# MLP of a decoder trunk: one more half product joined in the first stage, and the order of VectorE's additions in the last chunks

## The reference

```
def _squared_relu_mlp(h, w1, w2):
    return jnp.square(jax.nn.relu(h @ w1)) @ w2
for layer in range(DEPTH):           # DEPTH = 2
    h = _rms_norm(x, norm_mix_g[layer])
    x = x + mixer(h)                 # attention in layer 0, retention in layer 1
    h = _rms_norm(x, norm_ffn_g[layer])
    x = x + _squared_relu_mlp(h, ffn_w_in[layer], ffn_w_out[layer])
return _rms_norm(x, final_g)
```

## Time and profile before

| | us |
|---|---|
| median of 3 runs (1245.33 to 1245.84) | 1245.82 |
| the profiled execution, its own time | 1246.04 |
| its span, first to last instruction | 1244.2 |
| TensorE busy (PE), share of the span | 1233.8, 99% |
| VectorE busy (DVE) | 983.8, 79% |
| ScalarE busy (ACT) | 779.0, 63% |
| POOL busy | 297.0, 24% |

### The profile page before, as it was taken

How to read it: one execution, slowest core, us unless ns; L and a number is a source line. 1 busy time by engine, 2 the same in 40 slices (tenths; PEclk the granted TensorE clock), 3 DMA queues, 4 the chain that set the end, 5 groups by cost and what they waited for, 6 DMA issues and landing times.

```text
span 1244.2 us, 18372 instructions
## 1 busy us (share of the span) xinstructions
PE 1233.8 (99%) x6870; PEld 1064.4 (86%) x6870; DVE 983.8 (79%) x1280; ACT 779.0 (63%) x1088; POOL 297.0 (24%) x330
## 2 busy tenths in 40 slices
PE   9999999999999999999999999999999999999997
PEld 6788888898888988889898889898889888898886
DVE  6588647598889798898666797567898988979888
ACT  6688755477575675765656645556677747466474
POOL 2343653111211112101131212231231122111220
PEclk9999999999999999999999999999999999999999
DMA  7367567778988989874968597969589898889983
GB/s 246 98 135 165 134 152 193 206 204 195 226 212 229 228 184 231 216 224 111 226 138 188 137 232 170 220 153 233 99 224 245 209 202 218 228 221 210 226 202 107
DMA packets 147976, 238.89 MB, mean 192 GB/s; under 512 B 51104, under 2 KB 72872, under 8 KB 147888
## 3 DMA queue, kind: packets, MB, share of 16 engines
q0 software_dynamic: 32352, 102.79, 44.0%
q1 hardware_dynamic: 115232, 134.60, 34.1%
q10 hardware_dynamic: 304, 0.33, 0.1%
HBM read 127.57 MB, written 2.11 MB: 104 GB/s over the span
## 4 chain that ended last, share of the span: by engine, by line
PE 87%; DVE 6%; issue 2%; ACT 2%; DMA 1%; SPq 0%; POOLq 0%; POOL 0%; ACTq 0%; DVEq 0%
PE banks L1072 19%; PE banks L1452 11%; PE banks L1030 11%; PE banks L998 6%; PE banks L1520 6%; PE banks L1241 6%; PE banks L1041 6%; PE banks L1401 5%; PE banks L1181 4%; PE banks L1035 3%; PE banks L1466 2%; PE banks L1343 2%; PE banks L1208 2%; DVE w L2356 2%; PE banks L1415 1%
## 5 line engine op out<-in xcount | busy, mean ns | idle before, releaser
L2356 DVE TENSOR_TENSOR w<-raw_tiles,w 128x1024 fp32r<-128x1024 f32 x312 | 371.7, 1220 | 33.8 <-ACT w L1662 33.8
L1662 ACT ACTIVATE w<-raw_tiles 128x1024 fp32r<-128x1024 f32 x312 | 316.3, 1052 | 129.6 <-PE banks L1072 60.8
L1072 PE MATMUL banks<-w,arena_q 128*128 128x512 f32 x1332 | 305.2, 390 | 0.7 <-DVE x L2696 0.7
L3378 POOL DMA_DIRECT2D raw_tiles<-raw_tiles x176 | 152.3, 905 | 629.9 <-DVE w L2356 358.1
L1072 PEld LDWEIGHTS banks<-w,arena_q 128*128 128x128 f32 x1332 | 248.7, 188 | 53.9 <-DVE x L2696 2.0
L1452 PE MATMUL banks<-w,h_ops 128*128 128x512 f32 x672 | 154.0, 390 | 0.0
L1452 PEld LDWEIGHTS banks<-w,h_ops 128*128 128x128 f32 x672 | 125.6, 188 | 25.7
L1030 PE MATMUL banks<-h_ops,w 128*128 128x512 f32 x576 | 144.1, 392 | 0.0
L1030 PEld LDWEIGHTS banks<-h_ops,w 128*128 128x128 f32 x576 | 104.0, 189 | 18.8
L1041 PEld LDWEIGHTS banks<-h_ops,w 128*128 128x128 f32 x576 | 78.6, 190 | 5.6
L998 PE MATMUL banks<-h_ops,w 128*128 128x256 f32 x672 | 82.0, 283 | 0.0
(11 more groups left out here) (253 smaller groups left out, 1886.3 us busy)
## 6 DMA issues: line engine op xcount, KB each, us to landing
raw_tiles<-raw_tiles POOLq DMA_DIRECT2D x176, 512.0 KB, 5.6
raw_tiles<-in_ffn_w_in SPq DMA_DIRECT2D x64, 512.0 KB, 6.2
raw_tiles<-in_ffn_w_out SPq DMA_DIRECT2D x64, 512.0 KB, 6.1
raw_tiles<-in_odd_w_in SPq DMA_DIRECT2D x32, 512.0 KB, 5.3
raw_tiles<-in_even_w_in SPq DMA_DIRECT2D x48, 256.0 KB, 3.5
raw_tiles<-in_odd_w_in SPq DMA_DIRECT2D x32, 256.0 KB, 5.5
raw_tiles<-in_odd_w_out SPq DMA_DIRECT2D x16, 512.0 KB, 6.0
raw_tiles<-raw_tiles POOLq DMA_DIRECT2D x20, 256.0 KB, 4.1
```

What stands on the lines that cost most here:

```text
L1072: mm = pe.matmul(bank[first + t][:, :], a_ring[a_slot(g, i)][:, a, k, P * t:P * t + P], w_slots[use_slot(use)][:, b, k, :], start=(starts ...
L1662: nc.scalar.activation(w_flat(use_slot(use), 0, half), raws[tile][:, 1024 * half:1024 * half + 1024], ACT.Copy).then_inc(m_hi, 1)
L2356: nc.vector.tensor_tensor(w_flat(use_slot(use), 1, half), raws[use_tile(key)][:, 1024 * half:1024 * half + 1024], w_flat(use_slot(use), 0, ...
L3378: pool.dma_start(raws[dst][:, part], raws[src][:, part], accum_op=ALU.add).then_inc(t_made[value][half], 16)
```

## The change

In the first stage, half b = 0 of product 5 is joined as well (`WIDE` now lists pairs of product and half). Its sums in HIGH come on top of those of products 0 and 4, so `wide_x_cross(HIGH, 0)` waits for product 5 and stands directly before `wide_x(HIGH, 0)`, behind two weight remainders, instead of between the two LOW instructions of half 0. The two semaphores of the cross subtractions become one, counted in the new order.

In the second stage of the last chunks (g = 3 and 7), product 4's tile 0 is added before product 3's two tiles, not after them. In g = 3, product 5's tile 0 is added before the remainder of the next stage's first weights and the variance, not after. ScalarE's square of the first tile waits for product 3's addition, now the later one.

```diff
+ADD_ORDER = [(i, t) for i in (0, 1, 4, 5, 2, 3, 6) for t in range(2)]
+LAST_ORDER = [(0, 0), (0, 1), (1, 0), (1, 1), (2, 0), (2, 1), (4, 0), (3, 0), (3, 1), (4, 1), (5, 0), (5, 1), (6, 0), (6, 1)]
 def add_order(g):
-    return (0, 1, 2, 3, 4, 5, 6) if g % CHUNKS == CHUNKS - 1 else (0, 1, 4, 5, 2, 3, 6)
+    return LAST_ORDER if g % CHUNKS == CHUNKS - 1 else ADD_ORDER
 def added(g, i, t=1):
-    return 14 * g + 2 * add_order(g).index(i) + t + 1
+    return 14 * g + add_order(g).index((i, t)) + 1
-def add_before(g, i):
-    same = [key for key in ADDS[:ADDS.index((g, i))] if PRODUCTS[key[1]][3] == PRODUCTS[i][3]]
+def add_before(g, i, t):
+    same = [key for key in ADDS[:ADDS.index((g, i, t))] if PRODUCTS[key[1]][3] == PRODUCTS[i][3] and key[2] == t]
...
-WIDE = (0, 1, 2, 3, 4, 6)
+WIDE = [(i, b) for i in range(7) for b in range(2) if (i, b) != (5, 1)]
...
-                            if i in WIDE:
+                            if (i, b) in WIDE:
...
-                    act.wait_ge(p_added, added(CHUNKS * (norm // 2) - 1, 4, t))
+                    act.wait_ge(p_added, added(CHUNKS * (norm // 2) - 1, 3 if t == 0 else 4, t))
...
             def wide_x_cross(g, tokens, b):
...
-                dve.wait_ge(p_done, use_done(first_use(g, 4), b))
-                nc.vector.tensor_tensor(v, v, wide_part(4, b, HIGH), ALU.subtract).then_inc(low_cross if low else high_cross, 1)
+                dve.wait_ge(p_done, use_done(first_use(g, 4 if low or b else 5), b))
+                nc.vector.tensor_tensor(v, v, wide_part(4, b, HIGH), ALU.subtract).then_inc(x_crossed, 1)
             def wide_x(g, tokens, b):
...
-                dve.wait_ge(low_cross if low else high_cross, wide_count(g) + b + 1)
+                dve.wait_ge(x_crossed, 2 * wide_count(g) + (b if low else 3 - b) + 1)
...
                     for b in range(2):
                         wide_x_cross(g, LOW, b)
-                        wide_x_cross(g, HIGH, b)
+                        if b == 1:
+                            wide_x_cross(g, HIGH, b)
                         wide_x(g, LOW, b)
                     w_lo(stage, 6, 1)
                     w_lo(stage + 1, 0, 0)
+                    wide_x_cross(g, HIGH, 0)
                     wide_x(g, HIGH, 0)
                     wide_x(g, HIGH, 1)
...
                 w_lo_both(stage + 1, 5)
+                add_product(g, 4, 0)
                 if last:
                     add_product(g, 3, 0)
                     add_product(g, 3, 1)
-                add_product(g, 4, 0)
                 operand_lo(g, 6)
                 add_product(g, 4, 1)
...
                 if norm == 2:
-                    use_lo(("qk", 0, 0), 0)
+                    add_product(g, 5, 0)
                 variance(norm, 0)
...
-                add_product(g, 5, 0)
+                use_lo(("qk", 0, 0), 0)
                 normed(norm, 0)
```

More of the change, by code:

```diff
@@ L235, in products_done @@
     return use_done(second_use(g, i), t)
+ADD_ORDER = [(i, t) for i in (0, 1, 4, 5, 2, 3, 6) for t in range(2)]
+LAST_ORDER = [(0, 0), (0, 1), (1, 0), (1, 1), (2, 0), (2, 1), (4, 0), (3, 0), (3, 1), (4, 1), (5, 0), (5, 1), (6, 0), (6, 1)]
 def add_order(g):
-    return (0, 1, 2, 3, 4, 5, 6) if g % CHUNKS == CHUNKS - 1 else (0, 1, 4, 5, 2, 3, 6)
+    return LAST_ORDER if g % CHUNKS == CHUNKS - 1 else ADD_ORDER
 def added(g, i, t=1):
-    return 14 * g + 2 * add_order(g).index(i) + t + 1
-ADDS = [(g, i) for g in range(2 * CHUNKS) for i in add_order(g)]
-def add_before(g, i):
-    same = [key for key in ADDS[:ADDS.index((g, i))] if PRODUCTS[key[1]][3] == PRODUCTS[i][3]]
+    return 14 * g + add_order(g).index((i, t)) + 1
+ADDS = [(g, i, t) for g in range(2 * CHUNKS) for i, t in add_order(g)]
+def add_before(g, i, t):
+    same = [key for key in ADDS[:ADDS.index((g, i, t))] if PRODUCTS[key[1]][3] == PRODUCTS[i][3] and key[2] == t]
     return same[-1] if same else None
@@ L711, in trunk @@
         z_added = sem("z_added")
-        low_cross = sem("low_cross")
-        high_cross = sem("high_cross")
+        x_crossed = sem("x_crossed")
         last_copied = sem("last_copied")
@@ L2688, in add_product @@
             def add_product(g, i, t):
-                if add_before(g, i):
-                    dve.wait_ge(p_added, added(*add_before(g, i), t))
+                if add_before(g, i, t):
+                    dve.wait_ge(p_added, added(*add_before(g, i, t)))
                 dve.wait_ge(p_done, products_done(g, i, t))
```

## The result

| | before | after |
|---|---|---|
| median of 21 runs each | 1245.49 (1244.95 to 1247.12) | 1247.6 (1246.91 to 1249.39) |
| the profiled execution's own time | 1246.04 | 1247.95 |
| its span | 1244.2 | 1246.1 |
| mean granted TensorE clock | 0.999 | 0.998 |

The ratio after to before is 1.0017, its 95% interval 1.001 to 1.0024: 2.1 us slower, with an interval of about 1.2 to 3.0. The forecast was 0.9 slower, 1246.7. The sign was right, but the slowdown is more than twice the forecast one: 1247.6 lies outside the forecast's own range (1246.2 to 1247.2) and at the very edge of the wide one (1245.3 to 1247.6). The kernel before came out at 1245.49 here, 0.33 lower than the 1245.82 on which the forecast stands. So it is the sizes that have to be looked for.

A forecast was written before the change was run, and what follows sets the result against it. TensorE's pace was taken to bound nearly everything, VectorE's chain the end from 1201.96. Terms 0.91 - 0.11 + 0.12 = +0.92 on 1245.82 gave 1246.7, own range 1246.2 to 1247.2, wide range 1245.3 to 1247.6.

The forecast's parts named there:

- VectorE's late pair: Before product 6: two dependent HIGH subtractions, starting 0.73 apart, hold TensorE, so product 6 really starts 0.15 later.
- TensorE's saved 0.09: Product 5 in each joined chunk: TensorE saves 0.08 to 0.09 if nothing holds it.
- the waits won in g = 3: Second stage: TensorE wins 0.9 before products 5 and 6, waits it off before the next norm's tile turn, keeps 0.11.
- the tail: From 1201.96 to the end: only VectorE's chain sets the length; the dependent pair of additions adds 0.12.
- rival A: Whole kernel: TensorE's own stalls are what counts, so removing them gives -2.1, 1243.7; chance 12%.
- Rival B: Dependent VectorE pairs cost no more than independent ones: +0.03 per joined chunk, total within 0.1 of 1245.8; chance 17%.
- covered behind: Into the second stage: the operand remainder slips 0.25, hidden by 0.5 of cover before the load.
- Rival C: Later subtraction spills into the second stage, each chunk paying 0.45 or more: +2.7, 1248.5; chance 6%.
- part 2: Fourth chunk (g = 3), reordered additions: `normed` starts 0.11 earlier, -0.11; bounds -0.93 and +0.12.
- paid six times: Product 6 in six joined chunks: the 0.15 delay recurs in each, +0.91 in all.
- part 3: Last chunk (g = 7), same reorder: only the dependent pair of additions counts, +0.12; bounds -0.3 and +0.2.
- part 1: Half of product 5 joined in six chunks: product 6 0.15 later each, +0.91; bounds -0.54 and +1.8.

The follow-up runs named there:

- e2: Kernel before with the new order of additions alone, product 5 not joined and the HIGH cross in its old place: 1246.16, ratio 1.0006.
- e8: e1 with six tiny VectorE instructions added at the start of VectorE's list: 1246.69, ratio 1.0007.
- e4: Changed kernel with the HIGH cross subtraction of half 0 moved between the two weight remainders, so one remainder splits the dependent pair: 1246.62, ratio 1.0009.
- e3: Changed kernel with the first tile's variance placed before product 5's addition in g = 3: 1246.65, ratio 1.0011.
- e1: Kernel before with half 0 of product 5 joined in six chunks, additions in the old order: 1247.06, ratio 1.0011.
- e7: e1 with 2 warm-up products instead of 9, meant to shift TensorE's instructions: 1248.06, ratio 1.0017.
- e9: Kernel before with the joined half alone, only in chunks g = 1, 2, 3 (layer 0): 1245.83, ratio 1.0003.
- e10: Kernel before with the joined half alone, only in chunks g = 5, 6, 7 (layer 1): 1246.16, ratio 1.0005.
- e5: Changed kernel with both HIGH subtractions of half 0 moved before the remainder of the second stage's first weights: 1247.93, ratio 1.0017.
- e6: e5 and e3 together, and product 3's two additions swapped in the last chunks: 1246.58, ratio 1.0009.
- e12: e6 with the joined half in every chunk but g = 5: 1245.41, ratio 0.9998.
- e11: e6 with no joined half, so the mended order alone: 1245.63, ratio 1.0.

## Why the prediction was right and wrong

**Right: which engine holds what.** That VectorE's late pair, not TensorE's saved 0.09, would set product 6; that the waits won in g = 3 would be waited off before the turn; and that the tail follows VectorE alone. Three waits are gone from TensorE (0.6, 0.3, 0.6), and the kernel isn't faster: rival A is out. e2 is the direct trial: it has all of the waits gone and no joined half, and is not faster.

**Right: the price of a joined half in its own chunk, 0.15.** Predicted as 0.73 for the dependent pair, 0.05 to the load and 0.11 for the first matmul that starts with its own load; found as 0.72, 0.05, 0.11 in five chunks, in g = 7 too once its late start is taken away (e8, 0.12). Rival B would have it at 0.03, and that is what the pair costs once it is no longer adjacent (e4, 0.02). The rule that I cited ("VectorE: DVE Perf Modes", "The DRAIN you can't avoid", in the Trainium skill) does not hold here as I read it: the dependent neighbour with its wait starts 0.12 later than an independent one, in the six chunks and in the tail.

**Right: it is covered behind.** The remainder of the first operand comes about 0.2 later in g = 1 (0.25 by my reckoning) and the second stage doesn't wait. Rival C named nearly the time that was measured, by a mechanism that isn't there.

**Wrong: part 2, "`normed` idled 0.15 for rstd, made by POOL from the late variance; now the remainder lies between".** I took POOL's row as 0.56 wherever it stands, and had the normed tile behind the remainder. Behind the new order POOL's instruction runs beside the remainder, takes 1.47 and ends 0.4 after it, and the normed tile idles 0.53 where I had 0: +0.48 (e2) instead of -0.11. This is the largest miss of the forecast. e3 changes this neighbour alone; the row is 0.56 again and about 0.6 comes back. The kernel before had the evidence, in the second norm, which I did not look at. POOL, then VectorE, of the kernel before:

```profile
912.61 1.47 POOL L3251 TENSOR_TENSOR rstd<-var,half_neg 128x1 f32<-128x1 f32 x1 [9.74 <-DVE var L2247]
915.61 0.55 POOL L3251 TENSOR_TENSOR rstd<-var,half_neg 128x1 f32<-128x1 f32 x1 [1.53 <-DVE var L2247]
924.84 1.76 POOL L3251 TENSOR_TENSOR rstd<-var,half_neg 128x1 f32<-128x1 f32 x1
```

```profile
912.38 0.14 DVE L2247 TENSOR_SCALAR var<-ssum 128x1 f32<-128x1 f32 x1
912.44 1.22 DVE L2356 TENSOR_TENSOR w<-raw_tiles,w 128x1024 fp32r<-128x1024 f32 x1
914.18 1.28 DVE L2257 SCALAR_TENSOR_TENSOR h_f<-x,rstd,gain 128x1024 f32<-128x1024 f32 x1 [0.53 <-POOL rstd L3251]
```

This is the changed order's g = 3 to the hundredth: variance, remainder, 0.53 of idling. The Trainium skill, "SBUF — State Buffer", "Who interferes with whom", says that a VectorE instruction with two SBUF inputs contends with a GpSimd instruction that reads SBUF; the traces agree, in the kernel before, the changed one and e2, and e3 shows the other side.

**Wrong: "the offsets are the same in the last such chunk ... so it is paid six times".** The offsets are VectorE's and TensorE's queue, and those were the same; but in g = 7 one instruction of VectorE started 0.35 later than its release allows, and the new order has no slack in front of product 6 to take it. 0.32 more. e8 removes it by moving the place in the stream, and the record numbers above tie all such late starts to places 128 apart. That the fetch of the next instructions is what comes late there is my reading, and no run shows the fetch itself. The sizes fit it: TensorE's 55 packets of 16 KB stand against some 14,050 of its instructions, 64 bytes each, and queue 14 carries instruction packets of 8 KB, which is 128 such instructions; which engine a packet of queue 14 is for the traces don't say.

**Wrong: that all six payments reach the end.** Four do. My own part 2 has VectorE's queue set the turn of g = 3, and my part 3 has it set the tail; then a TensorE that is 0.15 late in front of them costs nothing there. e1, e7, e8 and e9, with the old order, have the 0.15 of g = 3 back at the turn. Behind g = 7, in the seven kernels in which product 6 is held, VectorE's queue in the tail is 0.17 to 0.18 less late than TensorE; in the other six it is within 0.02 of it. (e4 is among the seven though its chunk costs 0.02 only; why, stays open.) So part 1 comes to 0.91 - 0.15 - 0.17 = 0.59 at the end.

**Wrong: "No DMA or queue of SP or POOL is passed by anything moved".** It is true of the lists, but the loss of 0.33 in g = 5 comes through a DMA all the same: the landing of a weight sum depends on more than its issue. In my sum it was taken as fixed. What delays it is supported by three counts but by no trial: see below.

**Right: part 3, +0.12**, measured +0.12.

Put together: 0.59 + 0.48 (turn) + 0.12 as I would now size the parts, 0.33 (g = 5) and 0.32 (g = 7) that had no term: 1.84. What scatters between kernels is -0.43 at the start and +0.57 near 697, together +0.14, which makes 1.98; the span differs by 1.97. That the sum closes so well is partly luck, since the two scattering places could as well have added up. The wait near 697 is TensorE's for line 3063, and the kernel before has it too with 0.55 (line 3058); against the kernel before this place is 0.2 to 0.4 earlier in e1 to e4 and 0.3 later in e8, with no edit near it. e8 and e10 lose another 0.7 near 877 in the same way. I count these as scatter; their cause stays open.

**Supported, not tried: the landing in g = 5.** The half sum in question has a twin in each of the six chunks, the same transfer of 512 KB at the same place of the first stage. Over the 14 kernels that makes 84 transfers. In 76 of them the time from issue to landing is 4.50 to 4.60. The other eight are the late ones: 5.11 to 5.19 in the changed kernel, e1, e3, e4, e7 and e8, 6.74 and 6.41 in e5 and e6. All eight are in g = 5, and in all eight a packet with TensorE's next instructions (16 KB, on a queue of its own) starts while the transfer is under way, 4.36 to 4.73 after its issue. Of the 76 only g = 5 of e9 and e12 has a packet that starts behind the issue, and there it comes with it (0.03 and 0.12 after). e5 and e6 issue this half closer behind the one before (3.15 instead of 4.47), which by itself does nothing: in their other five chunks, with 3.15 or less too, it lands after 4.50 to 4.57. Closeness and packet together go with the 2 us.

Three more places in the same traces say the same. In the retention, at 708 and at 888, four such transfers of 512 KB are issued in a row. The second of them, in the 14 kernels at both places, lands 6.77 to 6.85 after its issue where no packet with TensorE's instructions starts meanwhile (14 cases) and 7.95 to 8.11 where one does (14 cases). Each kernel has one of each: before, e2, e10 and e11 are late at 888, the other ten at 708. So it is not the kernel that is slow, but the place that the packet meets. And the first weight sum near 920 lands after 4.53 to 4.55 in the four kernels without a packet starting in it and after 4.84 to 5.89 in the ten in which one starts 0.5 to 1.1 after the issue. The packet need not come late in the transfer, then. The kernel before had this evidence too: below is the DMA view of the kernel before from the second transfer's issue on for 6.8 us, first at 708.7, then at 888.2 (queue: packets, MB, share of 16 engines; then issues, KB each, median time to landing). The second has an instruction packet, and its four transfers take 9.0 and not 7.8.

```profile
q0 software_dynamic: 323, 1.19, 94.0%
raw_tiles<-raw_tiles POOLq DMA_DIRECT2D x4, 512.0 KB, 7.8
```

```profile
q0 software_dynamic: 314, 1.16, 92.7%
q8 instruction: 1, 0.02, 0.9%
...
raw_tiles<-raw_tiles POOLq DMA_DIRECT2D x4, 512.0 KB, 9.0
```

How the packets' times follow from the program I can't tell: e9 has one joined half less than e1 before this place, so 8 matmuls and 8 loads more, and its packet comes 4.7 earlier. The run that was to move the packet on purpose (e7) did not move it, and e9's packet was expected elsewhere than it came. So this is a coincidence in time, among 84 transfers of one kind and 42 at the other places without an exception if a packet that comes within 0.12 of the issue counts as none, and not a trial.

## What to carry to other kernels

When an instruction moves, ask what now runs beside it on the other engines, not only what stands before and behind it: here a tiny POOL operation beside a VectorE operation with two SBUF inputs lasted until 0.4 after that one's end, 1.47 and not 0.55. Look for the new order elsewhere in the old trace (same instructions, another layer) before pricing it; here it stood there with its number. Put a dependent pair of short VectorE operations apart, if a third is there to lie between (a weight remainder in e4, another tile's addition in e6). And before a loss on one engine is multiplied by the number of chunks, ask in each chunk which engine sets what comes behind: here two payments of six were not felt.

## What the runs showed of the hardware that I had not expected

- POOL's 128x1 operation takes 0.55 beside a VectorE operation that reads a bank, and 1.46 to 1.76 beside a 128x1024 one with two SBUF inputs, ending 0.4 after it.
- A held VectorE instruction started 0.44 to 0.46 after its release, instead of at most 0.16, at three records of its list and nowhere else in 14 kernels: 703, 1087 and 1599, whole multiples of 128 apart. With six instructions more ahead of it the same operation starts on time, and another one is late (e8).
- The same accumulating DMA of 512 KB landed 4.50 to 4.60 after its issue in 76 of 84 cases, and 5.1 to 6.7 in the eight in which an instruction packet started in it; at two other places 6.8 and 8.0, in 14 cases each. That the program's own instructions are traffic that can meet a transfer was no part of my sum.
